# The second block's attention: order of projections, rounds and convolution taps

## What is computed

```python
att_x = windowed_gqa(axial_rope(q), axial_rope(k), v, k_ctx, v_ctx, sink)   # 8 query heads, 2 key heads
# a tile of 128 queries sees its own and its neighbouring key tiles, and 256 context keys
p = softmax(concat([s_loc, s_ctx, s_sink]))
a, g = split(glu_in)                                   # conformer branch
u = depthwise_conv(a * sigmoid(g), w_31_taps) + bias
merged = sum(sigmoid(gate_i) * (branch_i @ w_branch[i]))
x = x + gate_x * (merged @ w_out)
```

## Time and profile before

| | |
|---|---|
| median of 3 executions | 3430.07 us (3425.69 to 3430.37) |
| the profiled execution | 3426.29 us, span 3424.2 us |
| TensorE matmul busy | 3234.0 us, 94% of the span |
| VectorE busy | 1758.0 us, 51% |
| ScalarE busy | 882.4 us, 26% |
| TensorE's mean granted clock | 0.976 of full speed |
| second block, first layer: projection, attention | about 1300 to 1456 us, 1456 to 1578 us |
| second block, second layer: projection, attention | about 2518 to 2631 us, 2631 to 2726 us |

### The profile page before, as it was taken

One profiled execution on the slowest core, in us unless ns is written; L12 is line 12 of the kernel. 1 busy time (PEld: TensorE's weight loads), 2 busy tenths in 40 slices (PEclk: granted clock), 3 DMA queues, 4 the chain that ended last, 5 costly groups with the idle time before them and its releaser, 6 DMA issues.

```text
span 3424.2 us, 36861 instructions
## 1 busy us (share of the span) xinstructions
PE 3234.0 (94%) x13516; PEld 2066.6 (60%) x13516; DVE 1758.0 (51%) x3507; ACT 882.4 (26%) x1774; POOL 285.3 (8%) x246
## 2 busy tenths in 40 slices
PE   7988988999998989999999999999999999999998
PEld 4743653788744545565555555555544665778887
DVE  2244225787723337866455453444467644554554
ACT  2241222344311211154232131111111623122212
POOL 1200430333101320000000000000000000000000
PEclk9989999999998999999999999999999999999999
DMA  8646877533446873101111112212222111223231
GB/s 275 221 137 215 325 275 239 178 94 86 126 156 226 346 269 92 37 19 48 37 37 49 50 45 67 56 56 56 68 63 62 36 49 50 74 62 86 82 92 62
DMA packets 418495, 394.01 MB, mean 115 GB/s; under 512 B 27888, under 2 KB 353648, under 8 KB 410896
## 3 DMA queue, kind: packets, MB, share of 16 engines
q1 hardware_dynamic: 384768, 348.01, 32.1%
q10 hardware_dynamic: 15120, 23.68, 2.1%
q0 software_dynamic: 18432, 19.98, 1.7%
HBM read 440.78 MB, written 31.52 MB: 138 GB/s over the span
## 4 chain that ended last, share of the span: by engine, by line
PE 60%; DVE 7%; DMA 2%; issue 1%; ACT 1%; DVEq 0%; POOL 0%; ACTq 0%; POOLq 0%
PE psum L739 37%; PE psum L724 6%; DVE arena L2149 3%; PE psum L1227 3%; PE psum L937 2%; PE psum L1312 2%; DMA ring<-in_w_branch 1%; PE psum L956 1%; DVE ring L2146 1%; PE psum L1382 1%; PE psum L1394 1%; PE psum L1337 1%; PE psum L1347 1%; DVE arena L2146 1%; ACT arena L1599 1%
## 5 line engine op out<-in xcount | busy, mean ns | idle before, releaser
L739 PE MATMUL psum<-arena,ring 128*128 128x384 f32 (+1 forms) x2592 | 748.7, 439 | 30.1 <-DVE psum L2146 16.3
L739 PEld LDWEIGHTS psum<-arena,ring 128*128 128x128 f32 x2592 | 490.6, 191 | 261.7 <-DVE psum L2146 28.1
L739 PE MATMUL psum<-hT,ring 128*128 128x384 f32 (+1 forms) x2176 | 623.2, 440 | 1.3 <-ACT scratch L1599 1.3
L739 PEld LDWEIGHTS psum<-hT,ring 128*128 128x128 f32 x2176 | 413.9, 190 | 191.1 <-issue 7.8
L1599 ACT ACTIVATE scratch<-psum 128x256 f32<-128x256 f32 (+1 forms) x408 | 174.6, 428 | 964.2 <-PE psum L739 819.3
L2146 DVE TENSOR_TENSOR ring<-ring 128x512 f32<-128x512 f32 (+1 forms) x336 | 215.9, 662 | 265.5 <-PE psum L739 260.4
L2146 DVE TENSOR_TENSOR psum<-psum,scratch 128x256 f32<-128x256 f32 (+1 forms) x328 | 155.8, 479 | 369.8 <-PE psum L739 268.4
L1599 ACT ACTIVATE arena<-psum 128x512 f32<-128x512 f32 (+5 forms) x417 | 195.9, 499 | 538.2 <-PE psum L724 184.9
L724 PE MATMUL psum<-hT,ring 128*128 128x512 f32 (+1 forms) x832 | 310.4, 534 | 12.2 <-DVE hT L2142 6.0
L1591 ACT ACTIVATE arena<-psum,cols 128x256 f32<-128x256 f32 (+3 forms) x280 | 131.5, 492 | 514.9 <-PE psum L937 193.2
L724 PEld LDWEIGHTS psum<-hT,ring 128*128 128x128 f32 x832 | 158.9, 192 | 163.2 <-issue 145.7
(11 more groups left out here) (265 smaller groups left out, 3625.8 us busy)
## 6 DMA issues: line engine op xcount, KB each, us to landing
ring<-in_w_in SPq DMA_DIRECT2D x172, 512.0 KB, 4.1
arena<-in_moe_w SPq DMA_DIRECT2D x44, 1536.0 KB
ring<-in_ada_w SPq DMA_DIRECT2D x96, 512.0 KB, 6.4
ring<-in_w_mod SPq DMA_DIRECT2D x48, 512.0 KB, 5.4
ring<-in_ssm_w_in SPq DMA_DIRECT2D x48, 512.0 KB, 5.4
ring<-in_w_branch SPq DMA_DIRECT2D x64, 256.0 KB, 3.3
hT<-in_moe_w SPq DMA_DIRECT2D x10, 1536.0 KB
ring<-in_moe_w SPq DMA_DIRECT2D x10, 1024.0 KB
```

The lines of the kernel that those rows point to most:

```text
L739: mm = nc.tensor.matmul(flat(bank_, nb), lhs[:, k, :], rhs(k), start=(start and k == 0), stop=(k == kd_ - 1), skip_group_check=True)
```

## The change

Five edits, all in the second block.

1. `ATT_AFTER`: query columns 0 and 1 are projected in chunk 1, columns 2 and 3 in chunk 2, so the last chunk's `cf_g` and `cf_a` end the projection stage. The rotations follow: keys' rotation and the values' transposes in chunk 1, `rot_q` 0 and 1 in chunk 2, 2 and 3 in chunk 3. VectorE rotates keys behind `conv(0)`, two query columns behind `conv(1)` and two behind `conv(2)`; ScalarE's `kd` copies come in chunk 2. Scores wait only for the two query columns that they read, a context tile's for none.
2. In the first layer the tiles go 4, 0, 1, 5, 2, 3. Fewer gate parts stand ahead of the rounds and one more near their end; in the second layer round 3 has none.
3. Chunk 3's taps: two or three behind each `att_norm` but the last two (24 in the first layer, 18 in the second), the rest two at a time behind C11 (`mid`) in the pairs.
4. In the second layer VectorE takes round 1's maxima behind round 0's normalisation and taps.
5. The first pair's P1 and P2 come ahead of the last `att_values`; its weight sums and T1, T2 ahead of the last normalisation. The context rows of the transposed probabilities move to the other half of the weight-sum buffer. The four final gate products (`z_apply`) come two by two inside and behind the first `combine`.

```diff
-        ATT_AFTER = [[("att_k", 0), ("att_v", 0)], [("att_q", 0)], [("att_q", 1)], [("att_q", 2), ("att_q", 3)]]
+        ATT_AFTER = [[("att_k", 0), ("att_v", 0)], [("att_q", 0), ("att_q", 1)], [("att_q", 2), ("att_q", 3)], []]
-            return range(6 if l == 0 else 4)
+            return (4, 0, 1, 5, 2, 3) if l == 0 else (0, 1, 2, 3)
...
-            return each[0:3] if r < 0 else each[r + 3:r + 4]
+            if l == 0:
+                return each[r + 1:r + 2]
+            return each[0:2] if r < 0 else [] if r == 3 else each[r + 2 - r // 4:r + 3 - r // 4]
...
                     def att_scores(n, j):
                         kt = key_tiles(n)
+                        for c in (2 * j, 2 * j + 1) if kt else ():
+                            eng.wait_ge(vector_done, pe.at(("roped", l, c)))
...
-                        if j:
+                        gate_parts(z_parts(l, r))
+                        if j and r + 1 < len(rounds):
                             att_values(n)
...
-                    pair(*todo[0], hT, ready="h")
+                    pair(*todo[0], hT, ready="h", between=lambda: att_values(rounds[-1][0]))
...
                     att_max(0, *rounds[0])
-                    att_max(1, *rounds[1])
+                    if cx:
+                        att_max(1, *rounds[1])
                     for r, (n, j) in enumerate(rounds):
                         att_norm(r, n, j)
+                        if r + 2 < len(rounds):
+                            taps(2 if cx and key_tiles(n) else 3)
...
+                        if r == 0 and not cx:
+                            att_max(1, *rounds[1])
                         if r + 2 < len(rounds):
                             att_max(r + 2, *rounds[r + 2])
+                        if r + 2 == len(rounds):
+                            w_sums(*todo[0])
+                            eng.wait_ge(tensor_done, ve.at(("full",) + jobname("pt2", l, n, j, 4)))
...
-                    combine(*todo[0])
+                    combine(*todo[0], late=lambda: att_gates(2))
+                    att_gates(0)
                     decay(0)
...
-                    combine(*todo[1], beside=taps)
+                    combine(*todo[1], mid=lambda: taps(2))
```

More of the change, by code:

```diff
@@ L2049, in _ @@
                     todo = pairs(l)
-                    copies(*todo[0])
+                    copies(*todo[0], beside=last_values)
                     ret_decay(0)
@@ L2185, in w_sum_4, with combine @@
                 tt(to[:, 2 * kd_:3 * kd_, :], ring[:, slot, kd_:2 * kd_, :], to[:, kd_:2 * kd_, :], ALU.subtract).then_inc(vector_done, ve.step(("S4", a)))
-            def combine(a, b, mid=None, late=None, beside=None):
+            def combine(a, b, mid=None, late=None):
                 nb = blocks(a)
@@ L3088, in _ @@
                     for c in (1, 2, 3):
-                        combine(*todo[8 + 2 * c], beside=taps if c == 1 else None)
+                        combine(*todo[8 + 2 * c])
                         sc_conv(c)
```

154 lines of the change are left out of this document (79 added, 75 removed).

## The result

The changed kernel took 3375.36 us (median of 4 executions, 3373.76 to 3379.58) beside 3427.88 us of the kernel before (4 executions, 3418.54 to 3430.37), a ratio of 0.9854 with a 95% interval of 0.9832 to 0.9875. Five more executions in a later batch gave 3375.15 us and 0.9859 (0.9841 to 0.9877). It is faster, as predicted, but by 48 to 53 us and not by 31. The time lies 9 us under the low end of the range.

A forecast was written before the change was run, and what follows sets the result against it. TensorE's matmuls fill 94% of the span, so only its waits and lowered clock can be won: 49 us, less 17.9 left or added, is 31. From 3426.3 or 3430.1 us that gives 3397, range 3384 to 3414 (own range 3386 to 3406).

The forecast's parts named there:

- All 16.8 us go: Pairs behind both attentions: TensorE's listed waits for VectorE's C22 combine, 7.6 and 9.2 us, all vanish.
- The waits left in the attentions: TensorE waits expected to remain in the attention rounds: 8.0 us in the first layer, 7.6 in the second.
- the replay: Hand replay of all attention rounds with profiled instruction lengths, giving remaining waits of 8.0 and 7.6 us.
- copy_1 of the second layer's second pair: ScalarE copy that P6 waits for, expected 0.3 us late in each layer, 0.6 in all.
- the one wait that matters: Second layer, ahead of round 0's transposes: a TensorE wait of 3.3 us, released by VectorE's maxima.
- Rival 1: Rounds' taps more often on the path: half leaves 11 us gain, 3419; a quarter 3409; chance 0.20 with rival 2.
- Rival 2: Waits in the attention don't move, only the pairs gain: 16.8 us, 3413; chance 0.20 together with rival 1.
- The clock will fall as it does there now: Second layer's beginning, behind the 3.3 us wait: TensorE's lowered clock costs 1.7 us more.
- Rival 3: Short waits strewn over the rounds hold TensorE at 1.2 GHz, making the kernel slower, up to 3484; chance 0.05.
- The taps' price: A tap on VectorE takes 1.06 us in the first layer, 0.79 in the second; 39.6 us in the rounds.
- the shortened end: End of the attention, under edit 5: a wait of about 1.0 us stays of 4.5, without a clock fall.
- The first layer's 3.3 us wait: First layer, wait for the first normalised head: shrinks from 3.3 to 0.6 us with the context's rounds first.

The follow-up runs named there:

- e1: Kernel before with only the pairs' three taps moved behind C11, from between the weight sums and C22: 3397.12 us, ratio 0.9924.
- f11: Changed kernel with edit 4 alone undone, round 1's maxima again ahead of round 0's normalisation in the second layer: 3372.36 us, ratio 0.9856.
- e2: Changed kernel without taps in the attention rounds; three per pair again between weight sums and C22, in 11 pairs: 3391.47 us, ratio 0.9912.
- e6: Changed kernel without taps in the attention rounds, three taps behind C11 in each of eleven pairs: 3367.21 us, ratio 0.9835.
- e8: Changed kernel itself, unaltered, executed again in a later batch: 3375.15 us, ratio 0.9859.
- e5: Changed kernel with edit 5 alone undone (last values, first pair's sums, gate products back in their old places): 3376.87 us, ratio 0.9864.
- f9: Changed kernel with its gate parts one round earlier, none between the last two rounds' transposes: 3386.10 us, ratio 0.9897.
- e7: Changed kernel with the first layer's tiles in the order 0 to 5 again: 3373.76 us, ratio 0.9855.
- e4: Kernel before with edit 1 alone (query columns ahead, rotations and kd copies with them): 3408.86 us, ratio 0.9960.
- e3: Changed kernel with round 1's maxima ahead of the three taps behind round 0's normalisation, second layer: 3370.08 us, ratio 0.9848.

## Why the prediction was right in direction and wrong in size

The prediction named the waits and why they go, and the sum was too small. Its terms against the stretches (the 10 us of clock split as the windows gave them, 4.1 and 5.9):

| term | predicted | measured |
|---|---|---|
| first projection and attention: 12.3 - 8.0 - 0.3 + 4.1 of clock | 8.1 | 11.0 |
| second: 10.0 - 7.6 - 0.3 + 5.9 - 1.7 | 6.3 | 10.4 |
| pairs, "All 16.8 us go" | 16.8 | 23.8 |
| ahead of the second block | 0 | 3.7 |
| sum | 31.2 | 48.9 |

Two steps failed, both in how much waiting was priced.

**The pairs' term** was mis-sized most, by 7.0 us. The step that failed took the idle time that the profile lists for what a wait costs: "All 16.8 us go". Start to start, each C22 wait cost 0.27 us more than was listed, whether 0.5, 0.8 or 1.5 us, which makes 21.2 us of 16.9. Beside that stand 0.7 us at places with no wait listed and 1.4 us of clock. e1 has that part alone.

**The waits left in the attentions** were sized too long by the replay: 8.0 and 7.6 us, and with the second pair's 0.3 each 8.3 and 7.9. All idle time that is left there, also of kinds that the prediction did not count, was 6.9 and 6.2. So 7.6 and 7.1 us of idle time went (14.5 to 6.9, 13.3 to 6.2) where the sum had 12.3 - 8.3 = 4.0 and 10.0 - 7.9 = 2.1. Part of that are small waits that I had left out, 2.2 and 3.3 us before: the 0.5 and 0.7 us ahead of `rot_q` went, and copy_1 of the second layer's second pair, priced as 0.3 us to lose, won 0.9. The replay foresaw single waits of up to 2.0 us in the first layer, and none is above 1.2. In the second layer it was right for the one wait that matters: 3.3 us forecast, 3.1 measured, released by the maxima, as the replay had it. The 1.5 us behind it were not there: VectorE was by then ahead of TensorE and waited for it, 3.23 us in the row shown with f11.

**The rivals.** Rival 1, the taps on the path, is true to a small part: by e2, e6 and e8 they cost 3.0 to 3.7 us in the first layer and 2.6 in the second, about a seventh of their 39.6 us. Rival 2, no gain in the attentions, falls: 21.4 us came from the projections and attentions.

**The clock.** It won 3.6 us in each layer against 4.1 and 4.2 forecast (5.9 - 1.7). "The clock will fall as it does there now" held in one of two executions. Rival 3 did not come: the clock was 1.00 in the middle and at the end of both attentions, with waits of 0.2 to 1.2 us in many of the rounds. The rule of the Trainium skill that spoke for it (TensorE: Matmul & The Clock Gate, "A second HAM failure mode: psum-queue depth-cycling"), that short idle gaps between groups of matmuls make the clock swing, does not show with gaps of this length: in the attentions of these traces each fall stands behind a wait of 2.1 us or more.

**The taps' price** was right by the rows. The changed kernel's second layer has two taps in 1.54 us (the row shown with f11), 0.77 each, against 0.79 in the sum. The estimate of 0.57 us, in proportion to columns, that I had worked out from the Trainium skill (VectorE: DVE Perf Modes, "The perf-mode tier table") was too low.

**Which edit did what** was in part put wrongly. Edit 5 was given the shortened end; undone, it costs 0.0 and 1.5 us (e5), while the gate part of edit 2 costs 4.7 and 5.9 to 8.3 (f9). Edit 4 was described as what holds the 3.3 us wait, but priced at nothing against its absence; undone, it gives 2.8 us (f11). The first layer's 3.3 us wait, which I saw shrink by edit 2's tile order, is as short without that order (1.3 us in e7), and the order costs 3.0 us. The columns don't remove it either (e4 has 3.3 us in both layers). What does, by the rows shown with e4, is that only one gate part instead of two (none in the first layer) stands between the scores of the first two rounds. That is edit 2 again. The sum has no term for it, and no run has it alone, so its price is open; f9 moves gate parts too, but in the second layer leaves these two where they are.

**The base.** 3430.1 us was at the upper end: in three later batches the kernel before had medians of 3422.5 to 3423.6. The sum fell 18 us short (31.2 against 48.9 in the profiled executions); the rest of the 22 us between 3397 and 3375 is in which executions the times are taken from. The 3.7 us ahead of the second block are of the same kind, since the same first block started it anywhere from 1293.4 to 1304.8 us. That it differs by 11 us between executions is seen and not explained; in the two extremes, e1 and e5, TensorE's idle time ahead of the second block was 95.8 and 99.8 us and the time lost to the lowered clock 51.2 and 56.4, so both take part.

## What to carry to other kernels

Take a wait's cost from start to start, in a place with the wait and in one without it, not from the idle time that is listed: here each wait cost 0.27 us more than listed, so many short waits are worth more than their sum. When an engine of the second rank gets filler work, give it to the gap that is there in every repetition (VectorE's 4.8 us behind C11) before spreading it over a chain that is nearly closed. And when a change has several edits, undo each by itself: here three pieces, the taps behind C11 (26 us alone, 22 to 23 of them not clock), the columns (14 alone) and one gate part's place (11 when undone), sum to 51, about the 48 to 53 us of the whole, while edit 5 was near nothing and two changes of order cost about 3 us each.

## What the runs showed of the hardware

TensorE's clock after one and the same wait is not fixed. Behind a wait of 3.1 us in the second attention it ran at 1.2 GHz in three profiles (after, e5, f9) and at 2.4 GHz in two (e8, e7). Behind 4.5 us it was at 1.2 GHz in all five cases (before, e1, e4, and both layers of f9), behind 3.2 to 3.3 us it fell in all nine (three each in before, e1 and e4), and in no profile did waits of up to 1.5 us in the attentions lower it. Behind a wait of about 2.1 us a gate part took 5.39 us in the kernel before and 3.72 in e1, whose next wait of 3.3 us did lower it; TensorE in e1's first attention:

```profile
1451.86 3.72 PE L1312 MATMUL psum<-hT,ring 128*128 128x256 f32 x16 [2.08 <-ACT arena L1599]
...
1469.82 3.65 PE L1337 MATMUL psum<-const,arena 128*128 128x128 f32 x16 [3.28 <-DVE arena L2142]
```

In the pairs the clock took 0 to 5.3 us of pairs 1 and 5.1 to 8.4 of pairs 2, with C22 waits or without them (pairs 1: 3.6 before, 3.6 after, 0 in e1, 5.3 in e3). Profiles whose pairs are the same program differ by it too: pairs 1 took 891.3 us in e5, 892.6 in e8 and 894.3 in f11, with 1.8, 3.4 and 5.3 us lost to the clock. So a difference of a few us between two stretches can be laid to an edit only where idle time or start-to-start times show it.

A wait of TensorE costs more than its listed idle time by a fixed amount: 0.27 us for each of the 16 C22 waits, listed at 0.48 to 1.54 us. The one wait of 3.09 us (e8 beside f11) delayed the transposes by 3.25, the same 0.16 more up to the start.
